# Norm factors as square root and reciprocal, and sums, a factor and a split at other places, in a two-network transformer kernel

## The reference

```python
def rms_norm(x, g):
    xf = x.astype(jnp.float32)
    y = xf * lax.rsqrt(jnp.mean(xf * xf, axis=-1, keepdims=True) + NORM_EPS)
    return (y * g.astype(jnp.float32)).astype(x.dtype)

def modulate(h, shift, scale):
    return h * (1.0 + scale) + shift

def swiglu(h, w_in, w_out):
    gate, up = jnp.split(h @ w_in, 2, axis=-1)
    return (jax.nn.silu(gate) * up) @ w_out
```

## Time and profile before

| | us |
|---|---|
| median of 3 runs | 2761.53 (2759.18 to 2763.89) |
| the profiled execution, its own time | 2760.29 |
| its span, first to last instruction | 2758.5 |
| TensorE busy | 2653.4 (96%) |
| VectorE busy | 1635.0 (59%) |
| ScalarE busy | 1146.8 (42%) |
| mean granted TensorE clock | 0.986 |

### The profile page before, as it was taken

One profiled execution on the slowest core, in us unless ns is written; L12 is line 12 of the kernel. 1 busy time (PEld: TensorE's weight loads), 2 busy tenths in 40 slices (PEclk: granted clock), 3 DMA queues, 4 the chain that ended last, 5 costly groups with the idle time before them and its releaser, 6 DMA issues.

```text
span 2758.5 us, 39866 instructions
## 1 busy us (share of the span) xinstructions
PE 2653.4 (96%) x16424; PEld 2341.2 (85%) x16424; DVE 1635.0 (59%) x2684; ACT 1146.8 (42%) x1775; POOL 0.3 (0%) x5
## 2 busy tenths in 40 slices
PE   7999899999999999999999999999999999998998
PEld 6999899999989998888874687888888888876998
DVE  6655677656666785556641555556665445576554
ACT  6455544545544453222242533323242322446443
POOL 0000000000000000000000000000000000000000
PEclk9999999999999999999999999999999999999999
DMA  5543477544355763445521024445534445331554
GB/s 180 181 139 115 156 234 225 185 134 160 124 176 182 226 210 129 151 140 160 164 81 61 24 69 130 137 152 158 156 118 150 138 147 170 111 130 55 172 181 129
DMA packets 113908, 402.81 MB, mean 146 GB/s; under 512 B 12352, under 2 KB 15552, under 8 KB 113600
## 3 DMA queue, kind: packets, MB, share of 16 engines
q1 hardware_dynamic: 113728, 400.26, 44.9%
HBM read 399.17 MB, written 1.05 MB: 145 GB/s over the span
## 4 chain that ended last, share of the span: by engine, by line
PE 90%; DVE 4%; ACT 4%; issue 1%; DMA 0%; SPq 0%; DVEq 0%; ACTq 0%
PE psum L558 26%; PE psum L560 26%; PE psum L559 26%; PE psum L905 3%; PE psum L939 2%; ACT L1212 1%; DVE wlo L1577 1%; ACT whi L1145 1%; PE psum L1006 1%; DVE arena L1631 1%; PE psum L980 1%; DVE HLO L1636 1%; PE psum L950 0%; PE psum L962 0%; DVE arena L2135 0%
## 5 line engine op out<-in xcount | busy, mean ns | idle before, releaser
L558 PE MATMUL psum<-HHI,whi 128*128 128x256 f32 (+1 forms) x3560 | 1143.4, 321 | 45.3 <-DVE HLO L1704 17.3
L559 PE MATMUL psum<-HLO,whi 128*128 128x256 f32 (+1 forms) x3560 | 1131.4, 318 | 0.0
L560 PE MATMUL psum<-HHI,wlo 128*128 128x256 f32 (+1 forms) x3560 | 1130.9, 318 | 0.0
L1577 DVE TENSOR_TENSOR wlo<-wring,whi 128x1024 fp32r<-128x1024 f32 x589 | 706.7, 1223 | 364.1 <-ACT whi L1145 361.9
L1145 ACT ACTIVATE whi<-wring 128x1024 fp32r<-128x1024 f32 x589 | 606.1, 1055 | 404.7 <-PE psum L560 388.5
L558 PEld LDWEIGHTS psum<-HHI,whi 128*128 128x128 f32 x3560 | 688.7, 193 | 99.3 <-issue 28.0
L559 PEld LDWEIGHTS psum<-HLO,whi 128*128 128x128 f32 x3560 | 689.0, 194 | 44.0 <-issue 1.4
L560 PEld LDWEIGHTS psum<-HHI,wlo 128*128 128x128 f32 x3560 | 688.4, 193 | 41.8
L558 PE MATMUL psum<-HIDHI,whi 128*128 128x256 f32 (+1 forms) x1122 | 368.9, 329 | 0.0
L559 PE MATMUL psum<-HIDLO,whi 128*128 128x256 f32 (+1 forms) x1122 | 368.1, 328 | 0.0
L560 PE MATMUL psum<-HIDHI,wlo 128*128 128x256 f32 (+1 forms) x1122 | 368.1, 328 | 0.0
(11 more groups left out here) (280 smaller groups left out, 1824.8 us busy)
## 6 DMA issues: line engine op xcount, KB each, us to landing
wring<-ffn_in SPq DMA_DIRECT2D x264, 512.0 KB, 4.2
wring<-mod_w SPq DMA_DIRECT2D x144, 512.0 KB, 4.4
wring<-ffn_out SPq DMA_DIRECT2D x96, 448.0 KB, 3.9
wring<-w_proj SPq DMA_DIRECT2D x66, 512.0 KB, 3.8
wring<-w_gate SPq DMA_DIRECT2D x64, 512.0 KB, 4.2
wring<-ffn_out SPq DMA_DIRECT2D x48, 512.0 KB, 4.3
wring<-w_up SPq DMA_DIRECT2D x20, 512.0 KB, 3.5
wring<-w_out SPq DMA_DIRECT2D x16, 512.0 KB, 3.5
```

What stands on the lines that cost most here:

```text
L558: mm(out_, w[0], a[0], start=start, stop=False)
L559: mm(out_, w[0], a[1], start=False, stop=False)
L560: return mm(out_, w[1], a[0], start=False, stop=stop)
L1577: TTN(wlo[:, i, :], wring[:, raw_slot(tag, k), :], whi[:, i, :].bitcast(F32), ALU.subtract).then_inc(sem("weights_lo"), 1)
```

## The change

The factor becomes a square root on ScalarE (`root`, one table, loaded ahead by `root_table`) and a reciprocal in place on VectorE (`invert`), which waits for its own end (`ln`) before the next instruction. All 28 calls go this way; at the two factors of 512 columns in the first branch one `invert` takes both, so there are 16 reciprocals of 256 columns, 8 of 512 and 2 of 1024. The program has 53 table loads in place of 79.

In the halved norms four places change: the sum of half 0 stands inside the first lot of the second pass instead of behind it; the sum of the other half stands one block later; on both engines the split that stood in front of the first factor stands behind the first blocks; and on ScalarE the second factor stands in front of the last rounded copy of half 0. The sum of the context half of ("b0", 0) stands one lot later. In `ret_dve` a wait for the factor of the branch before is gone.

```diff
@@ TensorE: where the sums stand
-                        if s_ == one_ and c == 2:
+                        if s_ == one_ and c == 3:
                             half_sum(norm, two)
...
-                    if norm == ("b0", 0) and k == 12:
+                    if norm == ("b0", 0) and k == 13:
                         half_sum(norm, 1)
...
                         for c in range(a, b):
                             last = mm3(bank_of(tkey)[:, 0:SEQ], (w[0][:, c - a, :], w[1][:, c - a, :]),
                                        (hi[:, c, seqs(s_)], lo[:, c, seqs(s_)]), c == 0, c == FT - 1)
+                            if s_ and c == 4:
+                                half_sum(norm, 0)
                         if s_:
                             lot_event(last, tag_out, k)
-                            if k % 3 == 0:
-                                half_sum(norm, 0)
...
+                            if (s_, k, c) == (1, 5, 4):
+                                half_sum(("b2", 0), 0)
@@ ScalarE: the factor
-            def logarithm_table():
-
-                A(SPARE[:, 0:1], one, ACT.Ln)
+            def root_table():
+
+                A(SPARE[:, 0:1], one, ACT.Sqrt)
...
-            def rsqrt(out_, bank_key, n, count, name, key):
+            def root(out_, bank_key, n, count, name, key):
 
                 act.wait_ge(*done("filled", bank_key))
-                bank = bank_of(bank_key)
-                out_ = flat(out_)
-
-                A(out_, bank[:, 0:n], ACT.Ln, bias=eps, scale=1.0 / count).then_inc(*freed(bank_key))
-                act.wait_ge(*done("free", bank_key))
-                A(out_, out_, ACT.Exp, scale=-0.5).then_inc(*mark(name, key))
+                A(flat(out_), bank_of(bank_key)[:, 0:n], ACT.Sqrt, bias=eps, scale=1.0 / count).then_inc(*freed(bank_key, name, key))
@@ ScalarE: half_tail
-                split_ahead(tag, lots_[0])
                 half_factor(norm, 0)
                 half_hi(norm, 0, range(2), l, n3)
+                split_ahead(tag, lots_[0])
...
-                half_hi(norm, 0, range(3, KT), l, n3)
+                half_hi(norm, 0, range(3, KT - 1), l, n3)
                 half_factor(norm, 1)
+                half_hi(norm, 0, range(KT - 1, KT), l, n3)
                 half_hi(norm, 1, range(KT), l, n3)
@@ VectorE
+            def invert(buf):
+                ln(v.reciprocal(buf, buf))
...
                 v.wait_ge(*done("factor", (tag, s_)))
+                invert(R[:, seqs(s_)])
@@ VectorE: half_tail
-                split_ahead(tag, lots_[0])
                 v.wait_ge(*done("factor", (norm, 0)))
+                invert(R[:, seqs(0)])
...
                 r(1)
+                split_ahead(tag, lots_[0])
                 for m, key in zip(tiles_[:-1], keys):
                     second(m, key)
                 s(3)
                 r(2)
+                for m in tiles_[:-1]:
+                    add_square_half(norm, 1, m)
                 second(tiles_[-1], keys[-1])
                 s(4)
                 r(3)
-                for m in tiles_:
-                    add_square_half(norm, 1, m)
+                add_square_half(norm, 1, tiles_[-1])
...
                 v.wait_ge(*done("factor", tag))
+                invert(R[:, 0:n])
...
                     v.wait_ge(*done("fox_r", (l, 1)))
+                    invert(t1["RF"])
...
                 v.wait_ge(*done(f"{name}_r", l))
+                invert(buf["OQ"])
...
                 v.wait_ge(*done("ssd_r", l))
+                invert(d1["OQ"][:, 0:2, :])
...
                     v.wait_ge(*done("mla_r", t // 4))
+                    if t in (0, 4):
+                        invert(b2["RM"][:, t // 4, :])
```

More of the change, by code:

```diff
@@ L1033, in mla_pe @@
                             lot_event(last, "mlao", k)
-                            if k == 5:
-                                half_sum(("b2", 0), 0)
             def swa_pe():
@@ L1159, in half_factor @@
             def half_factor(tag, s_):
-                rsqrt(R[:, seqs(s_)], ("ss", tag, s_), SEQ, D, "factor", (tag, s_))
+                root(R[:, seqs(s_)], ("ss", tag, s_), SEQ, D, "factor", (tag, s_))
             def half_hi(tag, s_, tiles_, l, n3):
@@ L1189, in residual @@
             def residual(tag, norm, n):
-                logarithm_table()
+                root_table()
                 tail = 3 if halved(norm) else 0
@@ L1295, in fox_act @@
                     for i in range(2):
-                        rsqrt(t1["RF"][:, 2 * i:2 * i + 2, :], ("ssf", l, i), 512, HD, "fox_r", (l, i))
+                        root(t1["RF"][:, 2 * i:2 * i + 2, :], ("ssf", l, i), 512, HD, "fox_r", (l, i))
                 if FOX_SCORES <= j < FOX_SCORES + HEADS:
@@ L1337, in gla_act @@
                 gate_step(l, "gss")
-                rsqrt(g1["OQ"], ("gss", l), 512, HD, "gla_r", l)
+                root(g1["OQ"], ("gss", l), 512, HD, "gla_r", l)
             def head_values(l, okey, buf, name):
@@ L1355, in ret_act @@
                 gate_step(l, "rss")
-                rsqrt(r1["OQ"], ("rss", l), 512, HD, "ret_r", l)
+                root(r1["OQ"], ("rss", l), 512, HD, "ret_r", l)
             def ssd_act(l):
@@ L1371, in ssd_act @@
                 gate_step(l, "yss")
-                rsqrt(d1["OQ"][:, 0:2, :], ("yss", l), 512, 256, "ssd_r", l)
+                root(d1["OQ"][:, 0:2, :], ("yss", l), 512, 256, "ssd_r", l)
             def merge_act(l):
@@ L1404, in mla_act @@
                 for part, count in ((0, 512), (1, 256)):
-                    rsqrt(b2["RM"][:, part, :], ("mss", part), 512, count, "mla_r", part)
+                    root(b2["RM"][:, part, :], ("mss", part), 512, count, "mla_r", part)
                 for t in range(12):
@@ L1515, in _ @@
             for l in range(DEPTH):
-                rsqrt(R[:, 0:SEQ], ("ss", ("n1", l)), SEQ, D, "factor", ("n1", l))
+                root(R[:, 0:SEQ], ("ss", ("n1", l)), SEQ, D, "factor", ("n1", l))
                 norm_hi(("n1", l), SEQ)
@@ L1527, in _ @@
                 residual(f"wo{l}", ("n2", l), SEQ)
-                rsqrt(R[:, 0:SEQ], ("ss", ("n2", l)), SEQ, D, "factor", ("n2", l))
+                root(R[:, 0:SEQ], ("ss", ("n2", l)), SEQ, D, "factor", ("n2", l))
                 norm_hi(("n2", l), SEQ)
@@ L1540, in _ @@
                 if l:
-                    rsqrt(R[:, 0:n], ("ss", ("b2", l)), n, D, "factor", ("b2", l))
+                    root(R[:, 0:n], ("ss", ("b2", l)), n, D, "factor", ("b2", l))
                     norm_hi(("b2", l), n, l, 2)
                 ffn(f"ffi2{l}1", f"ffo2{l}1", ("b2", l), n, *((("b0", 1), BOTH) if l == 0 else ("final", SEQ)))
-            rsqrt(R[:, 0:SEQ], ("ss", "final"), SEQ, D, "factor", "final")
+            root(R[:, 0:SEQ], ("ss", "final"), SEQ, D, "factor", "final")
         @block.vector
@@ L1870, in ret_dve @@
                 v.wait_ge(*done("rotary", 1))
-                v.wait_ge(*done("gla_r", l))
                 ln(rope(r1["K"], PJ[:, RQ + 2:RQ + 4, :], COS, SIN, r1["TC"], r1["TS"]))
@@ L2041, in ffn @@
                                 v.wait_ge(*done("factor", (norm, 1)))
+                                invert(R[:, seqs(1)])
                             for i in (2 * m - 8, 2 * m - 7):
```

## The result

The changed kernel takes 2777.05 us (median of 4 runs, 2775.97 to 2777.49) against 2761.27 for the kernel before (4 runs). The ratio is 1.0055, with a 95% interval of 1.0043 to 1.0066: 15 us slower, where 13 were forecast. The profiled execution took 2777.32 us, with a span of 2775.5 and a mean granted clock of 0.982, where it was 0.986.

What follows compares the result with a forecast made beforehand. TensorE was taken as the bound, busy 2653.4 us, 96% of the span; only idle time could move. Terms 2.2 - 3.6 + 8.0 + 2.6 + 3.25 + 0.3 = +12.8 us on 2760.3 gave 2773, about 2774 as median; range 2738 to 2797.

Steps and rivals of the forecast that it cites:

- The price of a column: Wide reciprocal on VectorE: 6 ns per column taken, between bounds of 1.05 and 13 ns; 1.68 us for 256 columns.
- eight passes: Rival for VectorE's reciprocal: eight passes per column, 8.4 ns, giving +32 us, 2793; chance 0.2.
- Plain norms: Six unhalved norms: root and reciprocal path 2.19 us in place of 1.76, +0.43 at five places, +2.2 us.
- Halved norms: Four norms done in two halves: second half's first matmul at 1405.65 against 1406.62, -0.95 us each, -3.6 in all.
- at about 1402.35: Halved norm: when VectorE ends the first half, after 8.5 us of work and about 1.8 us of waits for ScalarE.
- in front of the sum partly replaced by one in front of block 3: Halved norm: TensorE's wait before the second half's sum, 1.08 us, partly moves to before block 3.
- First branch: Score matmuls wait for the 1024-column reciprocal: +2.3 us plus 1.7 us of clock, taken as +4.0 per layer, +8.0.
- Gated branch: Factor inside this mixer: reciprocal lengthens VectorE's chain to a waiting matmul, +1.3 us per layer, +2.6 in all.
- compressed queries: Second network, once: reciprocal stands in front of four products TensorE already waits 4.1 us for, +3.25 us.
- state branch: Factor inside this mixer: Exp and its load (1.95 us) fall off, 3.25 come on; +0.15 per layer, +0.3 in all.
- The mixed norm: Norm between the networks: loses a short wait before the sum, gains a reciprocal on VectorE; taken as nothing, +-1 us.
- Exponentials: Exponentials that now need their own table load find ScalarE idle in front of them; no cost in the sum.

Runs made afterwards that it cites:

- cut in two: Changed kernel with the first branch's 1024-column reciprocal split into two halves, the keys' half one weight split earlier; 2772.54 us, ratio 1.0045 to the kernel before.

## Why the prediction was right, and where its steps were off

**The price of a column.** The step "I take 6 ns" held: 6.24. What was right by reasoning is that the surplus of the one-column reciprocal is paid for each column. That it was 6, and not 5 or 13, no row said, and since the bounds were 1.05 and 13 this choice decided the size and the sign: that it came so near is luck. The forecast weighed it against eight passes. The Trainium skill ("VectorE: DVE Perf Modes", "First, the fixed hardware budget") names a repeat count of 8; at the ordinary 1.05 ns that would be 8.4 ns, and the rows do not bear that reading out.

**Plain norms.** Predicted +2.2 us, measured +2.4 at the first blocks (0.67, then 0.42 or 0.43 four times), and with the split, not the root, as what the reciprocal stands behind. The rows gave a load 1.28 us, and with that the sum came out. The Trainium skill ("ScalarE: Activation LUTs", "What ACT_TABLE_LOAD costs") adds 1.38 us of drain; these norms would then have gained, and they lost. Behind the low clock that follows each of these stands, 0.7 us of the 2.4 are left. That is no finer measure: in the three kernels with Ln and Exp in the plain norms the last four of them together differ from before by -1.6, -0.9 and -0.4 us in the same way.

**Halved norms.** The mechanism was right, the term mis-sized: -0.95 each predicted; -1.40, -1.48, -1.40 and -1.40 measured at the first block, and 0.2 more behind two of them, where a stretch of low clock fell away: -6.0 in place of -3.6. (Four times -0.95 is -3.8; the sum has -3.6.) The failed step was the first half's end "at about 1402.35". In time from the first half's sum, that is 13.2 us; in the trace it is 12.7 (1405.22 to 1417.92), since VectorE waits 0.85 us in all for ScalarE's copies, and not the 1.8 assumed. Also the wait "in front of the sum partly replaced by one in front of block 3" was nearly absent: 0.23 us is listed.

**First branch.** Waits: +2.3 per layer predicted, 2.3 measured in both. Clock: the term taken from the earlier trace rows was 1.7 us per layer, and it was 4.5 and 3.2. That is the largest error of the sum, +4.3 us. The one stretch of low clock that was looked at, with 1.7 us of full speed lost, was taken as the price of any; here the clock stayed low for 10 and 7 us.

**Gated branch, compressed queries, state branch.** 2.6, 3.25 and 0.3 predicted; 2.9, 3.4 and at most 0.8 measured. Retention showed nothing to measure.

**The mixed norm.** "I take nothing, +-1 us": it gained 0.9.

**Exponentials.** "Exponentials that now need a load of their own find ScalarE idle" held. TensorE waits 2.79 for the first ones of the windowed attention where it waited 2.2, but they come at the same time (5.81 and 5.82 us behind the same matmul).

**The sum.** +12.8 was predicted against +17.0 in the profiled executions. The errors are -2.4 (halved), -0.9 (mixed), +4.3 (first branch's clock), about +2 (clock in other places), and about +1 from small terms. That the sum came within 4 us is in part luck: the halved norms gained too much and the clock cost too much.

**What stays open.** Why the clock stays low 7 to 10 us behind the scores. It did so behind waits of 2.96 and of 2.20 us alike, and stayed at 1.00 when the wait was gone. A wait between 0 and 2.2 us was not tried there. Open too is the low clock of the three places in the second network (+4.6 us): all but two of the nine kernels' traces have it at about that size, and one trace of the kernel before can't say whether it goes with the change.

## What to carry to other kernels

A reciprocal is paid per column and on VectorE, so in front of an engine that waits for VectorE it cost more here than the table load and the second step on ScalarE that it replaces; use it where ScalarE's chain ends last and few columns are needed. New places and a shorter factor belong together: here the places gave 0.1 to 0.2 us in each halved norm with Ln and Exp, and 1.4 with the root. A wait that has grown in a list is not yet a loss: look whether the work in front of it has become shorter. Where TensorE had no wait, a new one of 2 to 3 us can cost more in clock than in waiting: read the clock column behind it and not only the idle time. One stretch of low clock is no price list; take several rows before a term rests on it.

## What the runs showed of the hardware

- The reciprocal's 6.24 ns per column holds from 256 to 1024 columns. A multiplication and addition in place over the same columns took 291 ns for 256 and 686 for 1024, which is 0.51 ns per column, half of the 1.05 ns of the two-input operation in the earlier trace rows.
- A stand of TensorE does not always bring the clock down. Behind the 2.22 us wait at 1421.30 of the changed kernel it was 1.00 in every window to 1429, and behind an equal one at 2048.64 it was low from 2049.0 to 2052.4. In the kernel before it was low behind the 3.40 us wait of the earlier trace rows and stayed at 1.00 behind one of 3.42 at 1662.32. Behind the scores of the first branch, waits of 2.96 us in both layers and, cut in two, of 2.20 us were each followed by 7 to 10 us of low clock.
- Stretches of low clock lie in other places from one trace to the next where nothing changed near them. One at 1550 to 1554 is in the changed kernel, behind a wait of 1.74 us, and has no counterpart in the kernel before, behind the same wait at 1532.34; one of 6.8 us at 227 is in the kernel before and missing with only the places changed. One such stretch shifts a comparison by 1.5 to 3 us, and is why the effects of the norms, of 1 to 4 us, are told only roughly.
